# Reordering the mixing stage of a two-block transformer kernel: convolution first, attention and retention units between projection pieces

## The reference, cut to what matters

```
h = rms_norm_2(x, mix_norm[l])
z = h @ w_in[l]                                    # 256 x 3200
rq, rk, rv, rg, mq, mk, mv, ca, cg = split(z)      # 7 of 384, 2 of 256
y_ret  = silu(rg) * group_rms(retention(rotary(rq), rotary(rk), rv))   # 6 heads of 64
y_moba = softmax(causal(rotary(mq) rotary(mk)^T / 8)) mv               # 6 heads of 64
y_conv = silu(group_layernorm(causal_conv31(ca * sigmoid(cg)) + bias))
x = x + concat(y_ret, y_moba, y_conv) @ w_out[l]
```

## Time and profile before

| | |
|---|---|
| median of three executions | 4610.4 us (4602.6 to 4613.7) |
| the profiled execution's own time | 4619.2 us |
| its span, first to last instruction | 4617.4 us |
| mean granted clock | 0.93 |
| busy: PE, PEld, DVE, ACT, POOL | 84%, 53%, 62%, 25%, 19% of the span |
| mixing stage of layer 0, projection | 3673.2 to 3753.1 us |
| mixing stage of layer 0, units to YM's transposes | 3753.1 to 3819.3 us |
| mixing stage of layer 1, the same parts | 4236.4 to 4316.3, 4316.3 to 4382.5 us |

### The profile page before, as it was taken

The page is one execution under the profiler, slowest core; times in us unless marked ns, Lnnn a source line. Parts: engine busy times, 40 slices in busy tenths (PEclk is TensorE's granted clock), DMA queues, the critical chain, the costliest instruction groups (busy, mean ns, idle before and its releaser), DMA issues.

```text
span 4617.4 us, 42017 instructions
## 1 busy us (share of the span) xinstructions
PE 3876.7 (84%) x15093; PEld 2426.5 (53%) x15093; DVE 2869.2 (62%) x6620; ACT 1167.5 (25%) x2550; POOL 878.8 (19%) x772
## 2 busy tenths in 40 slices
PE   7789987777998669889896878777779989999898
PEld 1446554333654423334642554322228878998797
DVE  0342137796776777778887446786665565565665
ACT  1131011124111111122011321112114444444443
POOL 0000003341332233333333003444330000000000
PEclk9899998898999889999998988999999979999799
DMA  6212438996998899989998128999994434545253
GB/s 240 94 55 100 154 142 328 357 369 248 366 412 337 327 362 406 403 333 357 409 421 362 73 108 315 392 416 395 421 398 158 165 109 165 192 149 183 82 183 133
DMA packets 246622, 1225.88 MB, mean 265 GB/s; under 512 B 19257, under 2 KB 46203, under 8 KB 124429
## 3 DMA queue, kind: packets, MB, share of 16 engines
q0 software_dynamic: 110592, 805.36, 43.3%
q1 hardware_dynamic: 135820, 417.84, 24.3%
HBM read 1222.07 MB, written 1.05 MB: 265 GB/s over the span
## 4 chain that ended last, share of the span: by engine, by line
PE 42%; DVE 15%; DMA 15%; ACT 3%; issue 2%; POOL 0%; SPq 0%; DVEq 0%; ACTq 0%; POOLq 0%
PE ps L426 12%; PE ps L688 7%; PE ps L713 7%; PE ps L714 7%; PE ps L715 7%; DMA BIG<-in_t_uv,idx 5%; DMA gbuf<-in_t_uv,idx 5%; DMA wbuf<-in_t_uv,idx 4%; DVE gbuf L1661 2%; DVE BIG L1661 1%; DVE wbuf L1661 1%; DVE BIG L1654 1%; PE ps L419 1%; DVE gbuf L1828 1%; PE ps L414 1%
## 5 line engine op out<-in xcount | busy, mean ns | idle before, releaser
L426 PE MATMUL ps<-wbuf,BIG 128*128 128x512 f32 x1856 | 819.6, 599 | 14.6 <-DMA wbuf<-in_t_conv_out_w 6.2
L2466 POOL DMA_INDIRECT gbuf<-in_t_uv,idx x336 | 381.6, 1136 | 1709.3 <-DVE BIG L1626 931.0
L688 PE MATMUL ps<-gbuf,BIG 128*128 128x512 f32 x1016 | 515.6, 648 | 179.5 <-ACT BIG L1094 177.7
L1702 DVE TENSOR_TENSOR plo<-wbuf,phi 128x1024 fp32r<-128x1024 f32 (+1 forms) x344 | 401.1, 1180 | 326.7 <-ACT phi L1129 326.1
L426 PEld LDWEIGHTS ps<-wbuf,BIG 128*128 128x128 f32 x1856 | 355.2, 193 | 452.9 <-issue 441.0
L1661 DVE CUSTOM_DVE_ANT_0 gbuf<-gbuf,BIG 128x1024 f32<-128x1024 f32 x336 | 409.6, 1222 | 191.3 <-DMA gbuf<-in_t_uv,idx 190.5
L1109 ACT ACTIVATE BIG<-BIG 128x2 f32<-128x2 f32 x384 | 78.1, 203 | 1558.1 <-DVE BIG L1668 1553.7
L688 PEld LDWEIGHTS ps<-gbuf,BIG 128*128 128x128 f32 x1016 | 198.9, 205 | 461.9 <-ACT BIG L1094 247.7
L688 PE MATMUL ps<-wbuf,BIG 128*128 128x512 f32 x668 | 343.0, 651 | 113.7 <-ACT BIG L1094 113.7
L713 PE MATMUL ps<-XH,phi 128*128 128x256 f32 x1472 | 422.6, 287 | 18.2 <-DVE XL L1712 14.0
L1129 ACT CAST phi<-wbuf 128x1024 fp32r<-128x1024 f32 (+1 forms) x344 | 344.0, 1014 | 314.7 <-PE ps L715 314.0
(11 more groups left out here) (348 smaller groups left out, 5260.2 us busy)
## 6 DMA issues: line engine op xcount, KB each, us to landing
wbuf<-in_t_in SPq DMA_DIRECT2D x84, 1024.0 KB
wbuf<-in_t_w_mod SPq DMA_DIRECT2D x48, 1024.0 KB
wbuf<-in_ffn_wg SPq DMA_DIRECT2D x20, 2048.0 KB, 7.8
wbuf<-in_ffn_wu SPq DMA_DIRECT2D x20, 2048.0 KB, 8.8
wbuf<-in_t_conv SPq DMA_DIRECT2D x48, 768.0 KB
wbuf<-in_ffn_wd SPq DMA_DIRECT2D x16, 2048.0 KB, 7.9
wbuf<-in_t_peer_wq SPq DMA_DIRECT2D x24, 1024.0 KB
wbuf<-in_w_in SPq DMA_DIRECT2D x14, 1536.0 KB, 6.5
```

The source lines that it names most:

```text
L426: ins = p(mm)(bank, l, r, start=(k == 0), stop=(k == 7))
L688: ins = p(mm)(ps.of(("acc", T, tb, n)), dg, g[:, 1024 + n * 512:1536 + n * 512], start=(j == 0), stop=(j == last_on_pe(T, tb)))
L1702: v(tt)(lo, W2.of(key, rows_, n)[:, k0:k1, c0:c1], hi.bitcast(F32), ALU.subtract).then_inc(dve_piece.up(q), 1)
L2466: g(nc.gpsimd.indirect_dma_start)(slot, None, I["t_uv"], bass.IndirectOffsetOnAxis(ap=idx[:, tb % 3, j:j + 1], axis=0)).then_inc(g_landed[ ...
```

## The change

The stage keeps its computation. What moves:

- Tile 7 (convolution) comes first, and the second half of X is turned inside its first piece, as the feed-forward stages do it.
- The Z tiles follow in the order 4, 5, 6, 0, 1, 2, 3.
- Attention's units come before retention's. One unit step is issued after each piece of tiles 0, 1 and 2, two after each piece of tile 3 (`units_beside`, `in_turn`). What is left runs after the last piece. Output banks are claimed when their kind of unit begins, and Z's pair of banks is held while it fills.
- The taps are taken three after each piece of tiles 4, 5, 6 and two after each of 0, 1, 2. The rest comes before tile 3.
- `rotated` is split by kind of head: attention's in tile 6, retention's in tile 2, each for both token blocks, after that round's piece and in front of its unit. It has its own buffer `ro`. `turned` is split the same way, before tile 0 and before tile 3.
- The convolution's result is transposed and centred in tile 3. Its other end and both of retention's go to one `ends` after all units, with the roots together, then the gates.
- SP loads tile 7 first and the decay table in front of tile 3, then both halves of `w_out`.

```diff
+Z_ORDER = (4, 5, 6, 0, 1, 2, 3)
...
-            for n in (0, 1, 4, 5, 2, 3, 6):
-                if n == 6:
-                    turned(0)
-                    turned(1)
-                for kk in range(0, 8, 2):
...
-                    if n == 0 and kk == 4:
-                        pe_turn_half(p, M, 1, h_of)
-                        x_in(p, M, 1)
-                    x_in(p, M, 0)
...
-            for pair in range(2):
-                b = ps.claim(p, ("cz", M, pair), (dve_m2, (M, "cz", pair)))
...
-            ob = [ps.claim(p, ("ob", M, i), ((dve_m2, (M, "ret out", i)) if i < 2 else (dve_m2, (M, "att out", i - 2))))
-                  for i in range(4)]
-            ps.held |= {ps.where[("ob", M, i)] for i in range(4)}
+            def turned(qs):
+                for tb in range(2):
+                    for q in qs:
+                        z0 = (0, 384, 1536, 1920)[q]
+                        b = ps.claim(p, ("rt", M, tb, q), (act_m2, (M, "rt", tb, q)))
+                        p.wait_ge(*dve_m2.at(M, "rot", tb, q // 2))
+                        for j in range(3):
+                            ins = p(tr)(b[:, j * 128:(j + 1) * 128], Z[:, tb, z0 + j * 128:z0 + (j + 1) * 128], ident[:, :])
+                        ins.then_inc(pe_m2.up(M, "rt", tb, q), 1)
+
+            def out_bank(i):
+                ps.claim(p, ("ob", M, i), (dve_m2, (M, "ret out", i)) if i < 2 else (dve_m2, (M, "att out", i - 2)))
+                ps.held.add(ps.where[("ob", M, i)])
...
+            def unit_steps():
+                for i in (2, 3):
+                    out_bank(i)
+                yield from in_turn(mix2_units((0, 1)), att_scores, att_turn, att_values)
+                for i in range(2):
+                    out_bank(i)
+                yield from in_turn(mix2_units((None,)), ret_scores, ret_values)
+
+            for pair in range(2):
+                b = ps.claim(p, ("cz", M, pair), (dve_m2, (M, "cz", pair)))
+                for j in range(2):
+                    q, hi, lo = next_piece()
+                    p.wait_ge(*dve_piece.at(q))
+                    x_in(p, M, 0)
+                    new = None
+                    if pair == j == 0:
+                        def new():
+                            pe_turn_half(p, M, 1, h_of)
+                            x_in(p, M, 1)
+                    three(p, b[:, j * 256:(j + 1) * 256],
+                          [((hi[:, k, :], lo[:, k, :]), (XH[:, k, :], XL[:, k, :])) for k in range(8)],
+                          True, True, new).then_inc(pe_m2.up(M, "cz", pair, j), 1)
+                    piece_done(q, pe_m2, M, "cz", pair, j)
+                if pair == 0:
...
+                    pe_rms_rows(p, M)
+            steps = unit_steps()
+            for n in Z_ORDER:
+                if n == 0:
+                    turned((2, 3))
+                if n == 3:
+                    turned((0, 1))
                     b = ps.claim(p, ("ct", M), (dve_m2, (M, "ct")))
                     p.wait_ge(*dve_m2.at(M, "taps", 1))
                     cv = big.of(("cv", M))
                     for tb in range(2):
                         for cb in range(2):
                             ins = p(tr)(b[:, tb * 256 + cb * 128:tb * 256 + (cb + 1) * 128],
-                                    cv[:, cb * 256 + tb * 128:cb * 256 + (tb + 1) * 128], ident[:, :])
+                                        cv[:, cb * 256 + tb * 128:cb * 256 + (tb + 1) * 128], ident[:, :])
                     ins.then_inc(pe_m2.up(M, "ct"), 1)
-                if i in (7, 9):
-                    ps.held.discard(ps.where[("ob", M, (i - 7) // 2)])
+                bb = [ps.claim(p, ("z", M, n, tb), (act_m2, (M, "z", n, tb))) for tb in range(2)]
+                ps.held |= {ps.where[("z", M, n, tb)] for tb in range(2)}
+                for kk in range(0, 8, 2):
+                    q, hi, lo = next_piece()
+                    p.wait_ge(*dve_piece.at(q))
+                    for tb in range(2):
+                        tk = slice(tb * 128, (tb + 1) * 128)
+                        three(p, bb[tb][:, 0:384], [((XH[:, kk + i, tk], XL[:, kk + i, tk]), (hi[:, i, :], lo[:, i, :]))
+                                                    for i in range(2)], kk == 0, kk == 6).then_inc(pe_m2.up(M, "z", n, tb, kk), 1)
+                    piece_done(q, pe_m2, M, "z", n, 1, kk)
+                    if kk == 6:
+                        ps.held -= {ps.where[("z", M, n, tb)] for tb in range(2)}
+                    for _ in range(units_beside(n)):
+                        next(steps, None)
+            run(steps)
...
+            def ends():
+                for qb in range(2):
+                    sq = tmp.enter(a, ("rq", M, qb))[:, 0:384]
+                    a.wait_ge(*pe_m2.at(M, "rv", 5, qb))
+                    a(act)(sq, ps.of(("ob", M, qb))[:, 0:384], ACT.Square).then_inc(act_m2.up(M, "rq", qb), 1)
                 act_root(a, sts.of(("cv", M))[:, 8:16], dve_m2.at(M, "cmean"), act_m2, M, "croot")
+                for qb in range(2):
+                    act_root(a, sts.of(("rr", M, qb))[:, 0:6], dve_m2.at(M, "rmean", qb), act_m2, M, "rroot", qb)
+                for qb in range(2):
+                    s2 = tmp.enter(a, ("r2", M, qb))
+                    a(act)(s2[:, 0:384], Z[:, qb, 1152:1536], ACT.Silu).then_inc(act_m2.up(M, "rg", qb), 1)
+                s1 = big.of(("c12", M))[:, 0:512]
                 a.wait_ge(*dve_m2.at(M, "cln"))
-                a(act)(YM[:, 0:2, 768:1024], s1[:, 0:512].rearrange("p (b n) -> p b n", b=2), ACT.Silu).then_inc(
+                a(act)(YM[:, 0:2, 768:1024], s1.rearrange("p (b n) -> p b n", b=2), ACT.Silu).then_inc(
                     act_m2.up(M, "cy"), 1)
...
+            steps = unit_steps()
+            for n in Z_ORDER:
+                if n == 3:
+                    run(conv)
+                for kk in range(0, 8, 2):
+                    dve_next(v)
+                    if n == 6 and kk == 2:
+                        rotated(1)
+                    if n == 2 and kk == 2:
+                        rotated(0)
+                    if n == 3 and kk == 2:
+                        conv_turned()
+                    for _ in range(units_beside(n)):
+                        next(steps, None)
+                    for _ in range(3 if n > 3 else 2):
+                        next(conv, None)
+            run(steps)
+            ends()
...
+        def units_beside(n):
+
+            return {0: 1, 1: 1, 2: 1, 3: 2}.get(n, 0)
+
+        def in_turn(units, *stages):
+            for i in range(len(units) + len(stages) - 1):
+                for lag, stage in enumerate(stages):
+                    if stage and 0 <= i - lag < len(units):
+                        stage(units[i - lag])
+                yield
...
-            for n in (0, 1, 4, 5, 2, 3, 6):
+            for j in range(4):
+                pieces.append(((M, 7), 8, 512, (0, 8, j * 128, (j + 1) * 128), j == 3))
+            for n in Z_ORDER:
-            for j in range(4):
-                pieces.append(((M, 7), 8, 512, (0, 8, j * 128, (j + 1) * 128), j == 3))
...
-            for n in (0, 1, 4, 5, 2, 3, 6):
+            tile2(s, (M, 7), wi[:, 2688:3200], 512)
+            for n in Z_ORDER:
+                if n == Z_ORDER[-1]:
+                    tile2(s, ("decay", M), I["k_decay"], 256)
                 tile2(s, (M, n), wi[:, n * 384:(n + 1) * 384], 384)
-            tile2(s, (M, 7), wi[:, 2688:3200], 512)
-            tile2(s, (M, 8), wo[:, 0:512], 512)
-            tile2(s, ("decay", M), I["k_decay"], 256)
-            tile2(s, (M, 9), wo[:, 512:1024], 512)
+            for n in range(2):
+                tile2(s, (M, 8 + n), wo[:, n * 512:(n + 1) * 512], 512)
```

More of the change, by code:

```diff
@@ L1232, in conv_end, with unit_steps @@
                 a.wait_ge(*dve_m2.at(M, "cln"))
[L1233 removed]
+                a(act)(YM[:, 0:2, 768:1024], s1.rearrange("p (b n) -> p b n", b=2), ACT.Silu).then_inc(
                     act_m2.up(M, "cy"), 1)
[L1236 to L1247 removed]
+            def unit_steps():
+                yield from in_turn(mix2_units((0, 1)), att_scores, att_turn, None)
+                yield from in_turn(mix2_units((None,)), None, None)
@@ L1799, in dve_mix2_stage @@
                     dve_next(v)
+                    if pair == j == 0:
+                        dve_turn_half(v, M, 1, gain)
+                if pair == 0:
+                    dve_rms_rows(v, M, G)
             sg = big.claim(v, ("sg", M), (dve_m2, (M, "taps", 1)))
@@ L1834, in dve_mix2_stage @@
             dec = W2.of(("decay", M), 12, 256)
-            sums = [sts.take(("sums", M, qb), (dve_m2, (M, "att out", qb))) for qb in range(2)]
-            sts.held |= {sts.where[("sums", M, qb)] for qb in range(2)}
+            sums = [None, None]
             def ret_scores(u):
@@ L1888, in att_values, with conv_turned @@
                 sts.held.discard(sts.where[("sums", M, u.qb)])
-            def conv_end():
-                run(conv)
```

(24 more changed lines are left out.)

234 lines of the change are left out of this document (88 added, 146 removed).

## The result

| | before | after |
|---|---|---|
| median | 4612.0 us (4602.6 to 4616.3, 4 runs) | 4559.6 us (4556.6 to 4566.8, 4 runs) |
| the profiled execution's own time | 4619.2 | 4566.8 |
| mixing stage to YM's transposes, layer 0 and 1 | 146.1, 146.1 | 122.2, 122.9 |

The ratio is 0.9893, 95% interval [0.9879, 0.9907]: faster by 1.1%. The forecast was 4575 with a range of 4550 to 4604; 4559.6 lies at the low edge of its inner band (4558 to 4593) and 3 us above rival A's (4545 to 4557). The kernel after was later timed again beside two variants (run e11): 0.9886 [0.9867, 0.9905].

A forecast was written before the change was run, and what follows sets the result against it. TensorE bounds the projection, nothing cleanly the units' stretch at low clock. Terms sum to 128.0 a layer, 128.7 with the last wait, against 146.1: 17.4 saved, 35 in all, 4610.4 - 35 = 4575 us; range 4550 to 4604.

The forecast's parts named there:

- rival A: Mixing stage: TensorE alone is the bound, chain and rotation hide wholly; 4545 to 4557 us, chance 0.17.
- Entry: Stage start, convolution's four pieces first: as in the FFN entry, an idle 3.8 and low clock behind it; 19.1 us.
- Tiles 4, 5, 6: Twelve projection pieces after the entry, VectorE's subtract and three taps level with TensorE at 2.08 a piece; 25.0 us.
- 1.5 for VectorE to catch up: Behind tiles 4, 5, 6, at the first units: VectorE's leftover work costs 1.5 us.
- Rounds, claims and rotation: Tiles 0, 1, 2: rounds of 3.0 and 3.5 (39.0), PSUM claims 1.5, rotation's stall and clock 6.0 us.
- a loop of ScalarE and VectorE: Rounds of tiles 0, 1, 2: cast, subtract, scores, exponent, copy form a closed chain of 2.95 narrow, 3.5 wide.
- Rotation: Middle of tile 2, retention heads: 5.8 us on VectorE stalls TensorE about 3.9; 6.0 with the low clock.
- Tile 3: Last tile with transposes, four pieces and six retention units at full clock; 25.2 us, plus 0.7 for last values' wait.
- Ends: Behind all units: joint squares, roots, gates and last products with nothing covering them; 8.4 us.
- After the stage: Down projection: the 8 us pause leaves its first matmuls at the low clock; 1.0 us.
- Transfers: Second half of w_out, issued only after the last retention score: hidden, by little; uncovered, a late tile shows 1 to 4 us.
- rival C: Units' stretch: the clock stays low while units run, slower; kernel about 4673, with half of it 4605 to 4625; chance 0.08.

The follow-up runs named there:

- e11: The kernel after itself, unchanged, timed again beside two variants; ratio to the kernel before 0.9886.
- e2: The kernel after with the retention heads' rotation in four parts of two operations, one behind each unit of tile 2; ratio to the kernel before 0.9897.
- e1: The kernel after with all 21 unit steps behind tile 3 and none beside a piece; ratio to the kernel before 0.9981.

## Why the prediction was right

Faster was right, and the forecast lay 15 us above the median measured: 35 us of gain were forecast and 52 came. The stage's forecast of 127.7 (128.7 with 1.0 behind it) stands against 122.2 in layer 0. By its terms:

- **Entry** 19.1: 17.8. The mechanism, a pause (3.37 measured) and low clock behind it, was right. The comparison with the feed-forward was 1.3 too long: there the pause was 3.79 and 27 matmuls behind it ran at the low clock, here 3.37 and 15. In e11 the same stretch took 16.4.
- **Tiles 4, 5, 6** 25.0: 24.9, with TensorE and VectorE both full (24.90 and 24.12). The 1.5 for VectorE to catch up did not occur: TensorE has no wait until 0.34 us at the second unit.
- **Rounds, claims and rotation** 39.0 + 1.5 + 6.0 = 46.5: 45.8. The rounds were 3.0 and 3.54, as said, but for another reason, so the number was right by luck. I had TensorE's work at 2.8 and 3.35 and a loop of ScalarE and VectorE 0.15 longer. No row in the rounds waits, save 0.34 once and 0.77 once: TensorE itself fills them, 2.27 for a piece up to the unit's scores and 0.63 + 0.27 + 0.36 for the wide unit. The 2.08 of the prediction leaves out what a change between piece and unit costs on both sides. In this rival A was right; in that the rotation would hide it was not. The claims cost at most the 0.77.
- **Rotation.** Stall 3.9: 4.08. The transposes and values behind it cost 0.5 more at the low clock, the piece 1.4 (3.43 for 2.0): 6.1 from scores to scores over a common round, forecast 6.0. In layer 1 it is 6.8. e2 takes away just this.
- **Tile 3** 25.9 with the last wait: 24.8. The 2.0 for banks, leftover taps and jitter was 1 too much.
- **Ends** 8.4: 7.7, five table loads as said.
- **After the stage** +1.0: -0.5 and -0.3 against before. This reason was wrong. YM's 16 transposes take 3.2 us in both kernels, at the low clock both times, so the pause ahead of them lost nothing that was not lost already. Behind them the down projection started at the low clock before and at the full clock after. Windows of the transposes and of the down projection's start, before, then after:

```profile
3819.30:3822.70 3.40, 3.38 (x16) 3.26 (x16) 1.37 (x2) 1.73 (x3) 0.00 (x0) 0.50 0.02 5
3822.70:3824.10 1.40, 1.40 (x6) 1.15 (x5) 1.18 (x2) 1.13 (x3) 0.00 (x0) 0.54 0.00 0
```

```profile
3792.10:3795.50 3.40, 3.38 (x16) 3.26 (x16) 1.37 (x2) 1.72 (x3) 0.00 (x0) 0.52 1.05 387
3795.50:3798.00 2.50, 2.50 (x13) 2.05 (x12) 2.16 (x3) 1.57 (x3) 0.00 (x0) 1.00 0.29 107
```

- **Transfers.** No down piece waited for its weights.

The misses inside the stage add up to 5.5 in layer 0 and 4.8 in layer 1, with 1.5 and 1.3 behind it 13 in all: 4575 - 13 = 4562. Nearly all go the same way. The largest are allowances for waits that didn't come (1.5 for catching up, 0.7 of the 1.5 for claims, 1 in tile 3), the entry's low clock (1.3) and the clock behind the stage. What was right in mechanism is the main thing, the units at full clock between pieces and the rotation's stall; what was wrong in it are the loop that sets the rounds and the loss behind the stage.

Against rival C I leaned on the first block's attention, which runs at 1.00 with no dense pieces. e1 shows that this was a poor witness: the second block's units alone, without taps, ran at 0.54. Had the schedule left them alone, C's clock would have come. What kept the clock up was the pieces between, which e1 took away. Why the first block's attention keeps the full clock without pieces is open.

## What to carry to other kernels

Work made of small matmuls that wait for other engines is cheap between pieces of a dense projection and dear behind it: here the same units cost 20 us a layer more on their own. A long block on a helper engine (the rotation, 5.8 us on VectorE) that stands ahead of a unit's operation in its queue should be cut only where that engine has room in the next rounds; otherwise the wait moves by a stage, as in e2. And where a chain is served by rounds that one engine fills, adding an allowance for each possible queue wait biases the forecast to the slow side.

## What the runs showed of the hardware

The entry of the stage came out at one of two lengths for the same instructions. The pause ahead of the second half of X was 3.37 in one and 3.38 in the other, and what differs is the row behind it; the kernel after, then e11:

```profile
3675.85 0.55 PE L714 MATMUL ps<-XH,phi 128*128 128x256 f32 x1 [3.37 <-DVE XL L1729]
3676.19 0.42 PE L715 MATMUL ps<-XL,phi 128*128 128x256 f32 x1
3676.41 0.41 PE L716 MATMUL ps<-XH,plo 128*128 128x256 f32 x1
```

```profile
3667.09 0.36 PE L714 MATMUL ps<-XH,phi 128*128 128x256 f32 x1 [3.38 <-DVE XL L1729]
3667.28 0.28 PE L715 MATMUL ps<-XL,phi 128*128 128x256 f32 x1
3667.40 0.28 PE L716 MATMUL ps<-XH,plo 128*128 128x256 f32 x1
```

Matmuls start 0.21 apart there and 0.12 here: low and full level. S to T was 41.6 in four of the twenty layers traced in the table, 42.8 to 43.0 in the others. One pause of 3.4 us thus costs 1.4 us or nothing. Why it goes one way or the other is open.

Nothing ahead of the first mixing stage is touched by any of these kernels, yet the stage of layer 0 began between 3656.2 and 3670.6 in the ten executions of the table. This scatter of 14 us is 0.3% of the whole time and hides edits of a few us. Marks inside the stage leave it out, and that is why the readings above use them.
